# Gate and up of a SwiGLU on one NeuronCore: each weight tile as three 256-column matmuls into one place, instead of one of 512 and one of 256

## The reference

```python
x = _layer_norm(ALPHA * x + _dsa_mixer(x, *mix_p), ln1_g, ln1_b)
x = _layer_norm(ALPHA * x + (silu(x @ w_gate) * (x @ w_up)) @ w_down, ln2_g, ln2_b)
# x: (256, 2048)   w_gate, w_up: (2048, 5632)   w_down: (5632, 2048)
```

## Time and profile before

| | |
|---|---|
| median of 3 runs | 1012.62 us (1011.81 to 1013.52) |
| profiled execution, span from the first to the last instruction | 1010.0 us |
| TensorE matmul (PE) busy | 967.5 us, 96% |
| TensorE weight load (PEld) busy | 825.4 us, 82% |
| VectorE busy | 591.8 us, 59% |
| ScalarE busy | 504.0 us, 50% |
| granted TensorE clock, mean | 0.989 of full |

### The profile page before, as it was taken

One profiled execution on the slowest core, in us unless ns is written; L12 is line 12 of the kernel. 1 busy time (PEld: TensorE's weight loads), 2 busy tenths in 40 slices (PEclk: granted clock), 3 DMA queues, 4 the chain that ended last, 5 costly groups with the idle time before them and its releaser, 6 DMA issues.

```text
span 1010.0 us, 13692 instructions
## 1 busy us (share of the span) xinstructions
PE 967.5 (96%) x5070; PEld 825.4 (82%) x5070; DVE 591.8 (59%) x788; ACT 504.0 (50%) x712; POOL 85.0 (8%) x66
## 2 busy tenths in 40 slices
PE   6988999998999999999999999999999999999993
PEld 5877888886888888888888888888888888888882
DVE  5378885656995555555555555555555454544546
ACT  5465775345565555665444444444444343343441
POOL 0004550000750000000000000000000000000003
PEclk9999999998999999999999999999999999999997
DMA  8741433564255454545454555555548565564612
GB/s 324 285 167 42 153 103 131 199 250 166 89 212 200 171 203 169 204 167 200 174 195 178 189 185 186 188 180 194 197 144 324 165 215 182 182 214 165 225 66 83
DMA packets 27259, 183.49 MB, mean 182 GB/s; under 512 B 3168, under 2 KB 3168, under 8 KB 7648
## 3 DMA queue, kind: packets, MB, share of 16 engines
q1 hardware_dynamic: 27056, 183.12, 51.1%
q0 software_dynamic: 32, 0.00, 0.0%
q10 hardware_dynamic: 144, 0.02, 0.0%
HBM read 181.03 MB, written 2.10 MB: 181 GB/s over the span
## 4 chain that ended last, share of the span: by engine, by line
PE 91%; DVE 6%; ACT 1%; issue 1%; DMA 0%; POOL 0%; ACTq 0%; POOLq 0%
PE acc L1126 32%; PE acc L1028 31%; PE acc L1027 16%; PE acc L1043 4%; PE acc L1024 3%; PE acc L1025 1%; PE acc L1112 1%; PE tp L1171 1%; DVE score L704 1%; PE tp L1184 0%; DVE work L734 0%; DVE w_lo L647 0%; DMA raw<-in_x_t 0%; DVE xn L938 0%; DVE xn L926 0%
## 5 line engine op out<-in xcount | busy, mean ns | idle before, releaser
L784 DVE TENSOR_TENSOR w_lo<-raw,w_hi 128x1024 fp32r<-128x1024 f32 (+1 forms) x294 | 360.5, 1229 | 344.3 <-ACT w_hi L524 343.3
L524 ACT ACTIVATE w_hi<-raw 128x1024 fp32r<-128x1024 f32 (+1 forms) x294 | 304.2, 1037 | 397.6 <-PE acc L1028 224.0
L1028 PE MATMUL acc<-act_t,w_hi 128*128 128x512 f32 x1320 | 471.1, 399 | 0.0
L1027 PE MATMUL acc<-act_t,w_lo 128*128 128x256 f32 x1320 | 371.8, 282 | 0.2
L1028 PEld LDWEIGHTS acc<-act_t,w_hi 128*128 128x128 f32 x1320 | 248.2, 188 | 57.5
L1027 PEld LDWEIGHTS acc<-act_t,w_lo 128*128 128x128 f32 x1320 | 249.8, 189 | 4.2 <-DVE act_t L858 0.7
L1126 PE MATMUL acc<-w_hi,hid_t 128*128 128x512 f32 x704 | 216.7, 389 | 0.0
L1126 PEld LDWEIGHTS acc<-w_hi,hid_t 128*128 128x128 f32 x704 | 132.2, 188 | 27.3
L1126 PE MATMUL acc<-w_lo,hid_t 128*128 128x512 f32 x352 | 136.9, 389 | 0.0
L1126 PE MATMUL acc<-w_hi,o_t 128*128 128x512 f32 x256 | 81.3, 394 | 0.0
L1126 PEld LDWEIGHTS acc<-w_lo,hid_t 128*128 128x128 f32 x352 | 66.1, 188 | 13.8
(11 more groups left out here) (135 smaller groups left out, 764.1 us busy)
## 6 DMA issues: line engine op xcount, KB each, us to landing
raw<-in_w_gu SPq DMA_DIRECT2D x88, 1024.0 KB, 4.7
raw<-in_w_down SPq DMA_DIRECT2D x32, 1024.0 KB, 4.8
raw<-in_w_out SPq DMA_DIRECT2D x16, 1024.0 KB, 4.8
raw<-in_w_down SPq DMA_DIRECT2D x16, 768.0 KB, 4.2
raw<-in_w_in SPq DMA_DIRECT2D x7, 848.0 KB, 7.6
raw<-in_w_uq SPq DMA_DIRECT2D x4, 1024.0 KB, 4.8
raw<-in_w_ukv SPq DMA_DIRECT2D x4, 1024.0 KB, 4.7
ln_rows<-in_ln_rows SPq DMA_DIRECT2D x4, 1024.0 KB, 6.6
```

Source lines behind the costliest of these rows:

```text
L524: act.activation(w_hi[:, (2 * slot + half) % RING, 0:n], raw[:, slot, first:first + n], ACT.Copy).then_inc(hi_done, 1)
L784: dve.tensor_tensor(w_lo[:, h, 0:n], raw[:, slot, first:first + n], w_hi[:, h, 0:n], ALU.subtract).then_inc(lo_done, 1)
L1027: pe.matmul(acc[:, bank, 0:S], wl, rhs[:, 0, :], start=False, stop=False, skip_group_check=True)
L1028: return pe.matmul(acc[:, bank, :], wh, rhs, start=False, stop=stop)
```

## The change

`pair` is replaced in gate/up by `triple`, which issues three matmuls of 256 columns for each weight tile, all into the same 256 columns: x_hi w_hi, x_hi w_lo, x_lo w_hi. Gate takes columns 0 to 255 and up takes columns 256 to 511 of one bank, `2 * c`; the bank `2 * c + 1` is no longer used in this stage. Only the first matmul of the bank has the start flag. The sum of the three parts is complete in PSUM, so `ffn_low_step` and `ffn_combine` go; silu reads the gate half from PSUM, and the product reads the up half from PSUM. `sig` (now the storage of `low`) and `hid` get two places each. TensorE's wait at a tile's start is now for `ffn_hid`, the product of the tile two before, in place of `ffn_comb`. Attention's projections keep `pair`.

```diff
 (ScalarE)
-            def ffn_low_step(tile, c):
+            def ffn_silu_step(tile, c):
                 act.wait_ge(ffn_full, tile + 1)
-                act.activation(low[:], acc[:, 2 * c:2 * c + 2, S:2 * S], ACT.Copy).then_inc(ffn_low, 1)
-            def ffn_silu_step(tile):
-                act.wait_ge(ffn_comb, tile + 1)
-                act.activation(sig[:], comb[:, 0, :], ACT.Silu).then_inc(ffn_sig, 1)
+                act.activation(sig[:, c, :], acc[:, 2 * c, 0:S], ACT.Silu).then_inc(ffn_sig, 1)
...
                     hi_loop(used_ffn(tile - 1, j), R_FFN // RING + 1 + i, j % 2, 2 * c + j // 2)
-                    if j == 0 and older:
-                        ffn_silu_step(tile - 2)
                     if j == 1 and older:
-                        ffn_hi_step(tile - 2)
-                ffn_low_step(tile - 1, 1 - c)
+                        ffn_hi_step(tile - 2, c)
+                ffn_silu_step(tile - 1, 1 - c)
 (VectorE)
-            def ffn_combine(tile, c):
-                dve.wait_ge(ffn_low, tile + 1)
-                dve.tensor_tensor(comb[:], acc[:, 2 * c:2 * c + 2, 0:S], low[:], ALU.add).then_inc(ffn_comb, 1)
-            def ffn_mul(tile):
+            def ffn_mul(tile, c):
                 dve.wait_ge(ffn_sig, tile + 1)
-                dve.tensor_tensor(hid[:], sig[:], comb[:, 1, :], ALU.mult).then_inc(ffn_hid, 1)
+                dve.tensor_tensor(hid[:, c, :], sig[:, c, :], acc[:, 2 * c, S:2 * S], ALU.mult).then_inc(ffn_hid, 1)
...
                     if j == 0 and older:
-                        ffn_mul(tile - 2)
+                        ffn_mul(tile - 2, c)
                     if j == 1 and older:
-                        ffn_lo_step(tile - 2)
-                ffn_combine(tile - 1, 1 - c)
+                        ffn_lo_step(tile - 2, c)
 (TensorE)
+            def triple(bank, up, w, e0, k):
+                out = acc[:, bank, up * S:(up + 1) * S]
+                for x, part in ((0, w_hi), (0, w_lo), (1, w_hi)):
+                    last = pe.matmul(out, part[:, w, e0:e0 + P], act_t[:, k, x, :],
+                                     start=(k == 0 and up == 0 and x == 0 and part is w_hi),
+                                     stop=(k == KD - 1 and x == 1), skip_group_check=True)
+                return last
...
-                            last = pair(j % 2, j, (k % 8) * P, act_t[:, k, :, :], k == 0, k == KD - 1)
+                            last = triple(0, j % 2, j, (k % 8) * P, k)
...
-                    pe.wait_ge(ffn_comb, tile - 1)
+                    pe.wait_ge(ffn_hid, tile - 1)
...
-                        last = pair(2 * c + j // 2, j, n * P, act_t[:, k, :, :], k == 0, k == KD - 1)
+                        last = triple(2 * c, j // 2, j, n * P, k)
...
-                pe.wait_ge(ffn_comb, KF - 1 + c)
+                pe.wait_ge(ffn_hid, KF - 1 + c)
```

More of the change, by code:

```diff
@@ L136, in layer_kernel @@
         comb = sb("comb", [P, 2, S])
-        sig = sb("sig", [P, S])
-        hid = sb("hid", [P, S])
+        hid = sb("hid", [P, 2, S])
         stats = sb("stats", [P, TOK, COL_GROUPS * 6])
@@ L180, in layer_kernel @@
         ln2_rows = at(base_a)("ln2_rows", [P, 2, D])
+        sig = low
         ssq = small[:, 0:4]
@@ L260, in layer_kernel @@
         ffn_full = sem("ffn_full")
-        ffn_low = sem("ffn_low")
-        ffn_comb = sem("ffn_comb")
         ffn_sig = sem("ffn_sig")
@@ L565, in _, with ffn_hi_step @@
                                bias=ln1_gb[:, 1, k:k + 1]).then_inc(xt_hi, 1)
-            def ffn_low_step(tile, c):
+            def ffn_silu_step(tile, c):
                 act.wait_ge(ffn_full, tile + 1)
-                act.activation(low[:], acc[:, 2 * c:2 * c + 2, S:2 * S], ACT.Copy).then_inc(ffn_low, 1)
-            def ffn_silu_step(tile):
-                act.wait_ge(ffn_comb, tile + 1)
-                act.activation(sig[:], comb[:, 0, :], ACT.Silu).then_inc(ffn_sig, 1)
-            def ffn_hi_step(tile):
+                act.activation(sig[:, c, :], acc[:, 2 * c, 0:S], ACT.Silu).then_inc(ffn_sig, 1)
+            def ffn_hi_step(tile, c):
                 act.wait_ge(ffn_hid, tile + 1)
-                act.activation(hid_flat[:, bass.ds(tile * 2 * S, S)], hid[:], ACT.Copy).then_inc(ffn_hi, 1)
+                act.activation(hid_flat[:, bass.ds(tile * 2 * S, S)], hid[:, c, :], ACT.Copy).then_inc(ffn_hi, 1)
             def ffn_tile(c, i, older=True):
@@ L609, in _ @@
                 down_half(h, 0)
-                if h == 0:
-                    ffn_silu_step(KF - 2)
                 if h == 1:
-                    ffn_hi_step(KF - 2)
+                    ffn_hi_step(KF - 2, 0)
                 if h == 3:
-                    ffn_low_step(KF - 1, 1)
-                    ffn_silu_step(KF - 1)
-                    ffn_hi_step(KF - 1)
+                    ffn_silu_step(KF - 1, 1)
+                    ffn_hi_step(KF - 1, 1)
             with act.Fori(1, COL_GROUPS) as g:
@@ L866, in _, with ffn_lo_step @@
             dve.wait_ge(lo_done, 2 * R_FFN + 4)
-            def ffn_combine(tile, c):
-                dve.wait_ge(ffn_low, tile + 1)
-                dve.tensor_tensor(comb[:], acc[:, 2 * c:2 * c + 2, 0:S], low[:], ALU.add).then_inc(ffn_comb, 1)
-            def ffn_mul(tile):
+            def ffn_mul(tile, c):
                 dve.wait_ge(ffn_sig, tile + 1)
-                dve.tensor_tensor(hid[:], sig[:], comb[:, 1, :], ALU.mult).then_inc(ffn_hid, 1)
-            def ffn_lo_step(tile):
+                dve.tensor_tensor(hid[:, c, :], sig[:, c, :], acc[:, 2 * c, S:2 * S], ALU.mult).then_inc(ffn_hid, 1)
+            def ffn_lo_step(tile, c):
                 dve.wait_ge(ffn_hi, tile + 1)
-                dve.tensor_tensor(hid_flat[:, bass.ds(tile * 2 * S + S, S)], hid[:],
+                dve.tensor_tensor(hid_flat[:, bass.ds(tile * 2 * S + S, S)], hid[:, c, :],
                                   hid_flat[:, bass.ds(tile * 2 * S, S)], ALU.subtract).then_inc(ffn_lo, 1)
@@ L906, in _ @@
                     if g == 0 and h == 0:
-                        ffn_mul(KF - 2)
+                        ffn_mul(KF - 2, 0)
                     if g == 0 and h == 1:
-                        ffn_lo_step(KF - 2)
+                        ffn_lo_step(KF - 2, 0)
                     if g == 0 and h == 3:
-                        ffn_combine(KF - 1, 1)
-                        ffn_mul(KF - 1)
-                        ffn_lo_step(KF - 1)
+                        ffn_mul(KF - 1, 1)
+                        ffn_lo_step(KF - 1, 1)
                     if g > 0 and h in (2, 4):
```

## The result

The changed kernel takes 1022.24 us (median of 4 runs, 1021.55 to 1023.41) against 1012.21 us before (4 runs): a ratio of 1.0094, with a 95% interval from 1.0080 to 1.0109. It is 10 us slower. The prediction had 18 us faster as its likeliest case; the measured time is that of the near end of its rival 4, 1022.6 us.

The account below looks back on a forecast made before the run. TensorE's own stream in gate/up was taken to bound the kernel. A span of 1010.0 - 18.2 = 991.8 us, with 2.6 us for the median above it and other terms 0, gave 994.4 us; range 988 to 1023 us, 8 times in 10.

Parts of the forecast that it names:

- rival 4: In gate/up, each matmul has a fixed price beside its columns, so the third adds it: 1022.6 or 1049 us; chance 0.17.
- What bounds the kernel: In gate/up TensorE waits for nobody and everybody waits for it; its nanoseconds per weight tile decide.
- The stream of TensorE: Gate/up's three 256-column matmuls run at the uniform rate, 340 ns per weight tile against 352.9: 18.2 us gained.
- the 0.11 us between the two 256s at a bank's start: Gap from L1025 to L1027 in gate/up, taken to support 113.3 ns per uniform 256-column matmul.
- The excess of mixed streams: Streams of two sizes cost 3 to 4% more per column than uniform 512: 0.459 and 0.455 ns against 0.443.
- The value product at 110 ns: Six 128-column float32 matmuls, 110 ns each, as lower bound for a uniform 256: 5.28 us per bank, 32 us gained.
- Rival 3: In gate/up the weight load sets the pace, 0.117 to 0.119 us per 256-column matmul: 1010 to 1018 us; chance 0.17.
- Rival 5: Recorded 188 ns are real occupancy of one load path: 9.02 us per gate/up bank, +297 us; chance 0.02.
- the prediction's paragraph on the busy share of loads: The Trainium skill's rule would make loads the bound: 633 us of load for 488 us of gate/up.
- The fixed price on the page of the Trainium skill: At 2.5 ns per matmul, one more per weight tile would lose an estimated 3.5 us: 1016 us.
- The 2.6 us over the span: Amount by which the median time stands above the span, added to 991.8 us to give 994.4 us.
- The waits and the weights: TensorE's new wait for the product hidden, about 5.2 us early; gate/up's weight splitting and loads keep up: cost 0.

Follow-up runs that it names:

- e1_split: Kernel before with its evictions, the 512-column matmul against w_hi split into two of 256 in all tiles but the first: 1022.13 us against 1012.46.
- e7_wide: Changed kernel with gate/up matmuls at seven pairs of 32, 64 or 128 stationary and 256 to 512 streamed columns, six tiles each: 1307.5 us.
- e5_grouped: Kernel before with gate/up matmuls reordered throughout in blocks of eight of one size, then eight of the other: 1004.97 us against 1013.55, ratio 0.9921.
- e4_orders: Kernel before with gate/up's 512- and 256-column matmuls reordered into runs of 2, 8 and 16 in three stretches: 1007.66 us against 1012.46.
- e2_columns: Changed kernel with gate/up matmuls streaming 128 to 320 columns, seven widths of six tiles each, all with 128 stationary columns: 1027.78 us.
- e3_stationary: Changed kernel with gate/up matmuls at seven pairs of 32, 64 or 96 stationary and 128 to 256 streamed columns, six tiles each: 935.59 us.

## Why the prediction was wrong, point by point

- **What bounds the kernel: right.** Only TensorE's stream moved the time. The evictions taken away were worth nothing that can be measured (e1_split against the change), as the idle time in the earlier trace rows said. ScalarE's work fell by 48 us and not by 26: the table loads that went with the copy were not in the account.
- **The step that failed** is in "The stream of TensorE": "I take uniform sizes to run at the uniform rate per column: 3 x 113.3 = 340 ns per weight tile". A uniform 256 costs 120.0, not 113.3. The term was -18.2 us and measured +9.9 us (88 x 0.113). That was the sign.
- **Why it failed, in the rows.** Two rows seemed to agree on 113: half of a uniform 512, and the 0.11 us between the two 256s at a bank's start. The first halves a fixed price together with the columns: 226.7 is 213.3 and 13.3, and the 13.3 comes with each matmul and its full load (e7_wide). The second is the first 256 after a 512, which is cheaper than those after it (114, 119, 120 in e5_grouped). The very next gap of that group, 0.12 us (119 ns), was nearer the truth; the prediction counted it only in its rivals.
- **The excess of mixed streams** (0.459 and 0.455 ns per column against 0.443) was read as the price of mixing, which would go with uniform sizes. e4_orders shows that there is such a price, but of the 13.3 ns per pair over the uniform rate (353.3 - 340.0) it is only 6.7 (353.3 - 346.7), and the 512 bears it (236.4 for 226.7, while the 256 takes 116.9 for 120.0). The other 6.7 is half a fixed price: two matmuls carry the 768 columns, where the uniform 512 carries them in one and a half.
- **The value product at 110 ns**, the bound from below, is a floor of another kind. Its starts in the trace are 111 or 112 ns apart, and matmuls with 128 to 240 streamed columns take the same 111 to 112 ns with 128 stationary columns (e2_columns), less only with a shorter load (e3_stationary). It says nothing about where the stream itself is longer than the load.
- **Rival 4 was right** in mechanism, and at its near end in size: it gave 120 ns, 5.76 us per bank and 1022.6 us, against 120.0, 5.760 and 1022.24. The size was in part luck. Its 0.120 us came from the earlier trace rows, whose two gaps (119 and 121 ns) stand next to changes of size, and at the 40 bank starts of attention's projections the first such gap runs from 116 to 124 ns: no row of before showed a steady 256. The chance of 0.17 was low for a mechanism that fitted both mixed streams. The range, to 1023, held the time. Its far end, 126.2 ns, charged the 256 with what mixing costs the 512.
- **Rival 3** (the load sets the pace) is out as it was put: the load's floor is 112 ns, and the change did something. But load and stream lie close together at 256 columns, and the load's length has a share in the 120 there: with 64 stationary columns it is 113, which is no longer so at 320.
- **Rival 5, the recorded 188 ns as occupancy**, is refuted (the prediction's paragraph on the busy share of loads calls it rival 4 by mistake). The loads start 120 ns apart, nearly every one of them recorded as 192 ns long, and their busy share is 1.00. The Trainium skill (Perfetto Trace Analysis, Identifying the Most-Contended Engine) judges TensorE by the summed time of weight loads over the stretch. Here that sum is 4224 x 0.192 = 811 us in the 512 us of gate/up, 1.6 times the stretch, and the loads did not lengthen it to that.
- **The fixed price on the page of the Trainium skill** (TensorE: Matmul & The Clock Gate, Back-to-back issue gap) is 2.5 ns, given there for a matmul taken by itself; here it is 13.3 for these matmuls, each with its own load. By the page the loss would have been an estimated 3.5 us. The trace's price gives 1408 x 13.3 = 18.8 us for the third matmul, less the 1408 x 6.2 = 8.7 us that the mixing no longer costs (352.9 - 346.7), which is +10 us, as measured.
- **The 2.6 us over the span**, a term of the sum, were 0.8 too many: each run here stands 1.8 us above its own span (1022.21 and 1020.4, 1012.46 and 1010.7), and the rest was scatter between runs.
- **The waits and the weights**: cost 0, as forecast. TensorE has no wait for the product, which is 5.8 us early where about 5.2 were forecast.

**What stays open.** What the 13.3 ns are inside the engine. They don't depend on the place in PSUM, on accumulation, on the addresses tried or on the rows; at 256 streamed columns they shrink to 7 with 64 stationary columns but only to 11 with 32, at 320 they stay with 64, and at 512 they grow. No run streams without a load for each matmul. Why a change of size costs, why runs of 8 cost more than runs of 2, and why 448 columns cost 6.7 more than the line, is open as well.

## What to carry to other kernels

Price a matmul of another size by a line through steady runs of two or more sizes, never by scaling one size, and take no gap for steady that stands next to a change of size. In a stream that TensorE bounds, the same columns in fewer matmuls are cheaper, and evictions saved on engines that idle pay for nothing. Where a stream has two sizes, don't alternate them one by one: here runs of 16 alone gave 0.8%, and runs of 2 had most of that by the cadence (348.4 ns per pair against 347.9, from 352.9).

## What the runs showed of the hardware that was not expected

- Cadence with 128 stationary columns, steady: 111 to 112 ns for 128 to 240 streamed columns, 120.0 for 256, 125 for 272, 131 for 288, 146.7 for 320, 173.4 for 384, 206.7 for 448, 226.7 for 512, in fp32r with a load each, at the 2.4 GHz level.
- A beat is not always reached: at (64, 512) the starts are 224 to 236 ns apart all through the stretch, while at (128, 512) all but three are 226 or 227. Fewer stationary columns made the stream slower there, by about 3 ns.
- Mixing 512 and 256 columns costs, per pair over the 346.7 ns of the two among their own kind: 6.7 ns where they alternate one by one, 1.7 in runs of 2, 2.5 in runs of 8, 1.2 in runs of 16.
